# One hybrid mLSTM, convolution and cross-attention layer on one core: the 1152 tokens of a unit in pieces of 256, 512 and 384 columns instead of three times 384

## The chip, the cores and the metric

The kernel runs on 1 core of one Trainium2 chip. The metric is the device time of one execution in microseconds. The profile is of one execution on that core. TensorE's clock has two levels here, 1.2 and 2.4 GHz; the profile gives the granted share (1.00 is 2.4 GHz).

## What is computed

One layer of a streaming encoder, for a prompt of 1024 tokens and 8 sequences of 16 tokens, 1152 tokens of width 1024 in all, in float32. Cut to what matters here:

```python
def layer(x, ...):
    xn = rms_norm(x, g_mix_pre)
    q, k, v, o, ig, fg, glu, xq, gates = jnp.split(xn @ w_in, IN_SPLITS, axis=-1)   # 10248 columns
    y_ml = ...                                        # mLSTM, 4 heads x 256
    y_cv = jax.nn.silu(layer_norm(causal_dwconv(ga * sigmoid(gb), ...)))
    y_xa = mem_attention(xq, mk, mv)                  # into 256 memory tokens
    mixed = (sigmoid(gates[..., 0:D]) * (y_ml @ w_branch[0])
             + sigmoid(gates[..., D:2 * D]) * (y_cv @ w_branch[1])
             + sigmoid(gates[..., 2 * D:]) * (y_xa @ w_branch[2]))
    x = x + rms_norm(mixed @ w_out, g_mix_post)
    fa, fb = jnp.split(rms_norm(x, g_ffn_pre) @ w_ffn_in, 2, axis=-1)               # 2 x 2816 columns
    return x + rms_norm((silu(fa) * fb) @ w_ffn_out, g_ffn_post)
```

## The kernel before

**A unit.** Most products of the layer are done in units: 128 output features for all 1152 tokens. A unit's weights are 8 blocks (`KT`) of 128 by 128, its moving operand the activations `A_hi` and `A_lo`, held as 8 blocks of 128 partitions by 1152 tokens. To keep float32 accuracy, each operand is split into a high and a low part of type fp32r, and three products are summed: high by high, high weights by low activations, low weights by high activations. So a unit is 8 x 3 steps, and since a PSUM bank holds 512 columns, each step is one matmul for each of three pieces of the 1152 tokens: 72 matmuls, every one with its own weight load. `product` (line 256) writes these loops for all but the feed-forward part, where `in_unit` (line 1949) has them.

**Where the units are.** 1 unit for the two mLSTM gates (`pe_proj`, line 745), 80 units of the input projection (`pe_proj`), 3 x 8 units of the branch products (`pe_branch`, line 998), 44 units of the first feed-forward product (`in_unit`). That is 149 units. The feed-forward output (`out_part`, line 1971) and `w_out` (`wo_tile`, line 1923) work on 128 tokens by 512 columns and have another shape. The first phase projects the 256 memory tokens with matmuls of 256 columns, through `product` too (`pe_norm`, line 456).

**PSUM.** `PS` is all 8 banks of 512 columns. Units alternate between banks 0 to 2 and 3 to 5, and each of the three pieces starts at the start of its bank and fills 384 of its 512 columns (`banks`, line 742). The next unit computes while the one before is read out. What reads it takes all three pieces in one instruction, as a pattern of three runs of 384 (`thirds`, line 595): ScalarE's copies and tanhs of the projection (line 677), VectorE's gate products of the branches (lines 1028 and 1040), and in the feed-forward part ScalarE's tanh (line 2043) and VectorE's two products (lines 2162 and 2166).

**Order.** Every engine runs a list written out by hand, and semaphores tie them. `use_unit` (line 265) waits for the low part of the unit's weights (`w_lo_done`, made by POOL at line 253 from ScalarE's high part, line 249) and signals `w_used` with its last matmul. A unit writes its banks once the unit two before it has been read out. Between phases all engines meet (`end_phase`, line 269).

**The first unit of the branches.** The convolution's output goes through a LayerNorm that works on thirds of the tokens, `TC` = 384 columns each (`cut`, line 586). Its low parts are made by three instructions: thirds 0 and 2 by VectorE (`dve_ln`, line 935), third 1 by POOL (`pool_ln`, line 930). `pe_branch` takes the first unit (J = 0) piece by piece, 24 matmuls each: piece 0 waits for third 0, piece 1 for third 1, piece 2 for third 2.

```python
pe.wait_ge((ln_lo, ln_lo_pool, ln_lo)[c], (1, 1, 2)[c])
```

**The first units of the feed-forward part.** `in_unit(0, (0, 1), False)` and `in_unit(1, (0, 1), False)` compute pieces 0 and 1 of two units, and piece 2 follows once the last three tiles of 128 tokens are normalised.

Of the kernel before, what the change touches and what calls it, by code (L numbers as in the profile page):

```python
# [21 lines left out]
ACT = mybir.ActivationFunctionType  # L22
# [3 lines left out]
P = 128  # L26
# [5 lines left out]
NT = NTOK // P  # L32
NPT = SEQ // P
TC = NTOK // 3
H, DH = 4, 256
MEM = 256
CW = 31
# [48 lines left out]
def hybrid_step(nc, a, o):  # L86
    ctx = ExitStack()
    with ctx:
# [503 lines left out]

            return t[j] if isinstance(j, int) else t[bass.ds(j, 1)].rearrange("a p n -> (a p) n")

        def thirds(t):
            return t.rearrange("p (c n) -> p c n", c=3)

        def seg(t, n):

# [68 lines left out]
        def act_proj(act):  # L668
            def lap(i, func, scale, between=()):
                for s in range(RAW):  # L670
                    j = RAW * i + s
                    u = U_PROJ + j
                    split_hi(act, u + SPLIT, U_PROJ // RAW + i + (s + SPLIT) // RAW, (s + SPLIT) % RAW)
                    act.wait_ge(w_used, u + 1)
                    if not isinstance(j, int) or j > 1:
                        act.wait_ge(stage_stored[s % 2], 16 * (2 * i + s // 2))
                    nc.scalar.activation(thirds(stage[:, s % 2]), PS[:, 3 * (s % 2):3 * (s % 2) + 3, 0:TC], func,
                                         scale=scale).then_inc(p_copied, 1)
                    act.wait_ge(p_copied, j + 1)
                    act.dma_start(dtile(proj_d, j), stage[:, s % 2]).then_inc(stage_stored[s % 2], 16)  # L680
                    if s < len(between):
                        between[s](act)
# [51 lines left out]
                    split_lo(pool, U_PROJ + RAW * i + s + SPLIT, (s + SPLIT) % RAW)  # L734

        def a_hi(k, c):
            return A_hi[:, k, TC * c:TC * (c + 1)]

        def a_lo(k, c):
            return A_lo[:, k, TC * c:TC * (c + 1)]  # L740

        def banks(b):
            return [PS[:, 3 * b + c, 0:TC] for c in range(3)]

        def pe_proj(pe):
            pe.wait_ge(wif_lo_done, 1)
# [57 lines left out]
        def dve_proj(dve):  # L804
# [9 lines left out]
            steps.wait()  # L814
            dve.wait_ge(state_m_loaded, 48)
            dve.wait_ge(wif_used, 1)
            steps.mark(nc.vector.tensor_scalar(thirds(g_i[:]), PS[0:H, 3:6, 0:TC], g_bias[0:H, 0:1], None, ALU.add))
            nc.vector.tensor_scalar(thirds(g_f[:]), PS[32:32 + H, 3:6, 0:TC], g_bias[32:32 + H, 0:1], None, ALU.add).then_inc(gate_read, 1)
            dve.wait_ge(gate_read, 1)

            nc.vector.scalar_tensor_tensor(out=g_a[:], in0=g_f[:], scalar=-1.0, in1=g_f[:], op0=ALU.mult, op1=ALU.min).then_inc(g_dve, 1)
# [197 lines left out]
        def dve_branch(dve, n, between=None):  # L1019
            def body(i):  # L1020
                for s in range(RAW):
                    J = KT * n + RAW * i + s
                    lap = 2 * n + i
                    dve.wait_ge(w_used, U_BR + J + 1)
                    dve.wait_ge(gate_loaded[s % 2], 16 * (2 * lap + s // 2 + 1))
                    if not isinstance(J, int) or J > 1:
                        dve.wait_ge(part_stored[s % 2], 16 * (2 * lap + s // 2))
                    nc.vector.scalar_tensor_tensor(out=thirds(part_out[:, s % 2]), in0=thirds(gate_in[:, s % 2]), scalar=1.0,
                                                   in1=PS[:, 3 * (s % 2):3 * (s % 2) + 3, 0:TC], op0=ALU.add,
                                                   op1=ALU.mult).then_inc(part_mul if n else part_done, 1)  # L1030
                    if n:
                        dve.wait_ge(part_mul, J - KT + 1)
                        dve.wait_ge(prev_loaded[s % 2], 16 * (2 * (lap - 2) + s // 2 + 1))
                        nc.vector.tensor_tensor(part_out[:, s % 2], part_out[:, s % 2], prev_in[:, s % 2], ALU.add).then_inc(part_done, 1)

            def merge(k):
                J, b = 2 * KT + k, k % 2
                dve.wait_ge(w_used, U_BR + J + 1)
                dve.wait_ge(gate_loaded[b], 16 * (J // 2 + 1))
                nc.vector.scalar_tensor_tensor(out=thirds(gate2[:, b]), in0=thirds(gate2[:, b]), scalar=1.0,  # L1040
                                               in1=PS[:, 3 * b:3 * b + 3, 0:TC], op0=ALU.add, op1=ALU.mult).then_inc(part_mul, 1)
                dve.wait_ge(part_mul, J - KT + 1)
                dve.wait_ge(prev_loaded[k // 4], 16 * KT)
                nc.vector.tensor_tensor(Y[:, k], Y[:, k], gate2[:, b], ALU.add).then_inc(part_done, 1)
            if n < 2:
                br_laps(dve, n, body)
            else:
                for k in range(KT):
                    if k == KT - 1:
                        between(dve)  # L1050
                    merge(k)
# [870 lines left out]
        def pe_ffn(pe):  # L1922
# [23 lines left out]
                    last = nc.tensor.transpose(PS[:, b + k // 4, P * (k % 4):P * (k % 4 + 1)], Y[:, k, P * t:P * (t + 1)], ident[:])  # L1946
                last.then_inc(n_tx, 1)

            def in_unit(u, thirds_, end):
                pe.wait_ge(w_lo_done, IN_JOB[u] + 1)  # L1950
                pe.wait_ge(n_lo, 3 * thirds_[-1] + 3)
                if u == 0:
                    pe.wait_ge(n_st, NT - 1)
                elif u == 1:
                    pe.wait_ge(n_gn, NT - 1)
                elif u % 2 == 0:
                    pe.wait_ge(f_v, u // 2)
                else:
                    pe.wait_ge(f_g, u // 2)
                    for c in range(1, NC):  # L1960
                        if u == 2 * BASE[c] + 1:
                            pe.wait_ge(y_acc, NT * c - 1)
                for k in range(KT):
                    for n, (w_, m_) in enumerate(((w_hi, A_hi), (w_hi, A_lo), (w_lo, A_hi))):
                        for c in thirds_:
                            last = nc.tensor.matmul(PS[:, 3 * (u % 2) + c, 0:TC], w_[:, u % 2, k], m_[:, k, TC * c:TC * (c + 1)],  # L1966
                                                    start=k == 0 and n == 0, stop=k == KT - 1 and n == 2)
                if end:
                    last.then_inc(w_used, 1)
# [45 lines left out]
        def act_ffn(act):  # L2015
# [23 lines left out]
            def evac(u):  # L2039
                act.wait_ge(w_used, U_F + u + 1)  # L2040
                if u:
                    act.wait_ge(f_lo, u // 2)
                nc.scalar.activation(thirds(vb[:]), PS[:, 0:3, 0:TC], ACT.Tanh, scale=0.5).then_inc(f_th, 1)  # L2043

            def g_hi(m):
                act.wait_ge(f_g, m + 1)
# [83 lines left out]
        def dve_ffn(dve):  # L2130
# [27 lines left out]
            def gate(u):  # L2158
                dve.wait_ge(w_used, U_F + u + 1)
                if u % 2 == 0:  # L2160
                    dve.wait_ge(f_th, u // 2 + 1)
                    nc.vector.scalar_tensor_tensor(out=thirds(vb[:]), in0=thirds(vb[:]), scalar=1.0, in1=PS[:, 0:3, 0:TC], op0=ALU.add,  # L2162
                                                   op1=ALU.mult).then_inc(f_v, 1)
                else:
                    dve.wait_ge(f_v, u // 2 + 1)
                    nc.vector.scalar_tensor_tensor(out=thirds(vb[:]), in0=thirds(vb[:]), scalar=0.5, in1=PS[:, 3:6, 0:TC], op0=ALU.mult,
                                                   op1=ALU.mult).then_inc(f_g, 1)

            def collect(c, t):
# [162 lines left out]
```

## Time and profile before

| | |
|---|---|
| median of 3 runs | 2808.9 us (2807.84 to 2810.91) |
| profiled execution, its own time | 2810.57 us |
| its span | 2808.8 us |
| TensorE matmuls busy | 2686.7 us (96%), 15080 |
| TensorE weight loads busy | 2566.7 us (91%), 15080 |
| VectorE, ScalarE, GpSimd busy | 1087.8, 625.3, 650.2 us |
| mean granted clock | 0.985 |

PE is TensorE's matmuls, PEld its weight loads, which overlap them; DVE is VectorE, ACT ScalarE, POOL GpSimd, SP the engine that issues most transfers. A matmul's row in the profile is longer than the distance to the next one, since matmuls are pipelined: what one costs in a row of many is read from the starts.

### The profile page before, as it was taken

The numbers are of one execution on the slowest core, as the hardware profiler recorded it, in microseconds if no ns is written. First come the engines' busy times: TensorE is split into PE (matmuls) and PEld (weight loads), VectorE is DVE, ScalarE is ACT, GpSimd is POOL, SyncE is SP. The second block draws the span as 40 slices with busy tenths as digits, with TensorE's granted clock in tenths as the row PEclk, the third lists the DMA queues.
The fourth block names the chain that finished last, engine by engine and source line by source line (L and its number), as shares of the span: only waits on it lengthen the run. The fifth ranks groups of instructions, "written<-read, shape, count | busy, mean of one in ns | idle before, by whom it ended". The sixth has DMA issues, their size and how long they took to land.

```text
span 2808.8 us, 37457 instructions
## 1 busy us (share of the span) xinstructions
PE 2686.7 (96%) x15080; PEld 2566.7 (91%) x15080; DVE 1087.8 (39%) x1334; ACT 625.3 (22%) x912; POOL 650.2 (23%) x332
## 2 busy tenths in 40 slices
PE   5899999999999999899998898999999999999998
PEld 5899999999999999898888887988999998989897
DVE  3320199999962222216643342245220211110115
ACT  4331111111113233204521141024211110201021
POOL 5421212222221211221201120140313231404131
PEclk9999999999999999999999999999999999999999
DMA  6422333334252223244565534442202020202013
GB/s 180 144 88 88 106 129 121 110 108 142 91 186 80 96 79 105 98 160 106 135 209 177 175 130 147 163 137 90 75 23 68 29 63 23 68 16 68 13 40 135
DMA packets 286828, 294.96 MB, mean 105 GB/s; under 512 B 11386, under 2 KB 250322, under 8 KB 286704
## 3 DMA queue, kind: packets, MB, share of 16 engines
q1 hardware_dynamic: 271800, 239.91, 27.6%
q10 hardware_dynamic: 14912, 53.48, 4.8%
q8 instruction: 75, 1.23, 0.2%
q14 instruction: 41, 0.34, 0.0%
HBM read 208.27 MB, written 85.55 MB: 105 GB/s over the span
## 4 chain that ended last, share of the span: by engine, by line
PE 49%; issue 39%; POOL 8%; DVE 2%; ACT 1%; DMA 1%; SPq 0%; POOLq 0%; DVEq 0%; ACTq 0%
PE PS L1966 19%; PE PS L261 11%; PE PS L1989 9%; POOL w_lo L253 7%; PE PS L1936 3%; PE PS L1531 1%; PE PS L1550 1%; PE PS L1206 1%; PE PS L1214 1%; PE PS L1172 1%; DVE x_T L536 0%; PE PS L1179 0%; DVE y_T L1369 0%; DMA stage<-in_state_conv 0%; PE PS L1167 0%
## 5 line engine op out<-in xcount | busy, mean ns | idle before, releaser
L261 PE MATMUL PS<-A_hi,w_hi 128*128 128x384 f32 x2496 | 573.4, 336 | 17.3 <-DVE A_lo L935 10.0
L261 PE MATMUL PS<-A_lo,w_hi 128*128 128x384 f32 x2496 | 570.9, 335 | 0.0
L261 PE MATMUL PS<-A_hi,w_lo 128*128 128x384 f32 x2496 | 570.4, 335 | 0.0
L253 POOL TENSOR_TENSOR w_lo<-w_raw,w_hi 128x1024 fp32r<-128x1024 f32 x120 | 306.1, 2554 | 1052.6 <-ACT w_hi L249 1052.6
L261 PEld LDWEIGHTS PS<-A_hi,w_hi 128*128 128x128 f32 x2496 | 446.4, 188 | 20.1 <-issue 17.0
L261 PEld LDWEIGHTS PS<-A_lo,w_hi 128*128 128x128 f32 x2496 | 446.5, 188 | 0.0
L261 PEld LDWEIGHTS PS<-A_hi,w_lo 128*128 128x128 f32 x2496 | 446.2, 188 | 0.0
L890 DVE SCALAR_TENSOR_TENSOR c_out<-ext,taps,c_out 128x1024 f32<-128x1024 f32 x480 | 424.1, 962 | 0.7 <-DVE c_out L890 0.7
L249 ACT CAST w_hi<-w_raw 128x1024 fp32r<-128x1024 f32 x120 | 126.3, 1053 | 1079.2 <-PE PS L261 1071.8
L1966 PE MATMUL PS<-A_hi,w_hi 128*128 128x384 f32 x1056 | 242.5, 334 | 2.8 <-POOL w_lo L1881 2.8
L1966 PE MATMUL PS<-A_lo,w_hi 128*128 128x384 f32 x1056 | 242.3, 334 | 0.0
L1966 PE MATMUL PS<-A_hi,w_lo 128*128 128x384 f32 x1056 | 242.2, 334 | 0.0
L1966 PEld LDWEIGHTS PS<-A_hi,w_hi 128*128 128x128 f32 x1056 | 188.2, 188 | 3.5 <-POOL w_lo L1881 3.1
L1966 PEld LDWEIGHTS PS<-A_lo,w_hi 128*128 128x128 f32 x1056 | 188.4, 188 | 0.0
L1966 PEld LDWEIGHTS PS<-A_hi,w_lo 128*128 128x128 f32 x1056 | 188.4, 188 | 0.0
L1881 POOL TENSOR_TENSOR fo_lo<-w_raw,fo_hi 128x1024 fp32r<-128x1024 f32 x22 | 52.9, 2404 | 412.9 <-ACT fo_hi L1876 412.9
L1881 POOL TENSOR_TENSOR w_lo<-w_raw,w_hi 128x1024 fp32r<-128x1024 f32 x44 | 106.2, 2415 | 151.4 <-ACT w_hi L1876 151.4
L2162 DVE SCALAR_TENSOR_TENSOR vb<-vb,PS 128x1152 f32<-128x1152 f32 x22 | 29.8, 1354 | 272.8 <-ACT vb L2043 272.8
L1989 PE MATMUL PS<-fo_hi,G_hi 128*128 128x512 f32 x396 | 122.7, 391 | 0.0
L1989 PE MATMUL PS<-fo_lo,G_hi 128*128 128x512 f32 x396 | 122.0, 389 | 0.0
L1989 PE MATMUL PS<-fo_hi,G_lo 128*128 128x512 f32 x396 | 122.0, 389 | 0.0
L2173 DVE TENSOR_TENSOR Y_tok<-Y_tok,PS 128x1024 f32<-128x1024 f32 x45 | 54.9, 1221 | 153.6 <-PE PS L1989 153.0
(289 smaller groups left out, 2766.3 us busy)
## 6 DMA issues: line engine op xcount, KB each, us to landing
proj_d<-stage ACTq DMA_DIRECT2D x80, 576.0 KB, 2.7
w_raw<-in_w_in SPq DMA_DIRECT2D x80, 512.0 KB, 4.2
w_raw<-in_w_ffn_in SPq DMA_DIRECT2D x44, 512.0 KB, 3.9
w_raw<-in_w_branch SPq DMA_DIRECT2D x24, 512.0 KB, 4.3
w_raw<-in_w_ffn_out SPq DMA_DIRECT2D x22, 512.0 KB, 3.4
glu<-proj_d SPq DMA_DIRECT2D x16, 576.0 KB, 5.9
gate_in<-proj_d SPq DMA_DIRECT2D x16, 576.0 KB, 6.4
part_d<-part_out SPq DMA_DIRECT2D x16, 576.0 KB, 4.7
```

The source lines that it names most:

```text
L249: nc.scalar.copy(w_hi[:, s % SPLIT, 0:kt], w_raw[:, s, 0:kt]).then_inc(w_hi_done, 1)
L253: nc.gpsimd.tensor_tensor(w_lo[:, s % SPLIT, 0:kt], w_raw[:, s, 0:kt], w_hi[:, s % SPLIT, 0:kt].bitcast(F32), ALU.subtract).then_inc(w_lo_ ...
L261: last = nc.tensor.matmul(out, w[:, k], m(k, c), start=start and k == 0 and n == 0, stop=stop and k == kt - 1 and n == 2)
L890: steps.mark(nc.vector.scalar_tensor_tensor(out=c, in0=src, scalar=tap_scalar(w, k), in1=c, op0=ALU.mult, op1=ALU.add))
L1172: last = nc.tensor.matmul(PS[:, 0, P * h:P * (h + 1)], k_in[:, b, 2 * h + z], q_in[:, b, 2 * h + z], start=z == 0, stop=z == 1)
L1206: last = nc.tensor.matmul(PS[:, 4 + h, 0:E1], q_in[:, b, 2 * h + z], C_T[:, h, z], start=z == 0, stop=z == 1)
L1881: nc.gpsimd.tensor_tensor(l_, job_raw(n), h_.bitcast(F32), ALU.subtract).then_inc(w_lo_done, 1)
L1936: last = nc.tensor.matmul(PS[:, b + z], m_, w_[:, k, 512 * z:512 * (z + 1)], start=k == 0 and n == 0, stop=k == KT - 1 and n == 2)
L1966: last = nc.tensor.matmul(PS[:, 3 * (u % 2) + c, 0:TC], w_[:, u % 2, k], m_[:, k, TC * c:TC * (c + 1)], start=k == 0 and n == 0, stop=k == ...
L1989: last = nc.tensor.matmul(PS[:, b + z], g_[:, k, P * t:P * (t + 1)], w_[:, k, 512 * z:512 * (z + 1)], start=k == 0 and n == 0, stop=k == C ...
L2162: nc.vector.scalar_tensor_tensor(out=thirds(vb[:]), in0=thirds(vb[:]), scalar=1.0, in1=PS[:, 0:3, 0:TC], op0=ALU.add, op1=ALU.mult).then_i ...
L2173: nc.vector.tensor_tensor(Y_tok[:, t], Y_tok[:, t], pair(fo_banks(t)), ALU.add).then_inc(y_acc, 1)
```

## The change

A table `CUTS` gives the borders of the pieces: 0, 256, 768, 1152. The pieces are 256, 512 and 384 tokens wide. In PSUM a unit's 1152 columns lie without a gap: the first piece in the second half of its first bank, the second in the whole second bank, the third in the first 384 columns of the third bank (`wide`). Everything that reads a unit takes one run of 1152 columns. The order of matmuls, their number, their weights and the semaphores stay, but for the numbers in two waits that give the same value. The LayerNorm still works on thirds of 384, and `pe_branch` waits for the same semaphores ahead of its pieces.

```diff
+CUTS = (0, 256, 768, NTOK)
...
-        def thirds(t):
-            return t.rearrange("p (c n) -> p c n", c=3)
+        PS_cols = PS[:].rearrange("p b c -> p (b c)")
+
+        def wide(b):
+
+            return PS_cols[:, 1536 * b + 256:1536 * b + 256 + NTOK]
...
-                    nc.scalar.activation(thirds(stage[:, s % 2]), PS[:, 3 * (s % 2):3 * (s % 2) + 3, 0:TC], func,
+                    nc.scalar.activation(stage[:, s % 2], wide(s % 2), func,
                                          scale=scale).then_inc(p_copied, 1)
...
         def a_hi(k, c):
-            return A_hi[:, k, TC * c:TC * (c + 1)]
+            return A_hi[:, k, CUTS[c]:CUTS[c + 1]]
 
         def a_lo(k, c):
-            return A_lo[:, k, TC * c:TC * (c + 1)]
+            return A_lo[:, k, CUTS[c]:CUTS[c + 1]]
 
         def banks(b):
-            return [PS[:, 3 * b + c, 0:TC] for c in range(3)]
+            return [wide(b)[:, CUTS[c]:CUTS[c + 1]] for c in range(3)]
...
-                    nc.vector.scalar_tensor_tensor(out=thirds(part_out[:, s % 2]), in0=thirds(gate_in[:, s % 2]), scalar=1.0,
-                                                   in1=PS[:, 3 * (s % 2):3 * (s % 2) + 3, 0:TC], op0=ALU.add,
+                    nc.vector.scalar_tensor_tensor(out=part_out[:, s % 2], in0=gate_in[:, s % 2], scalar=1.0,
+                                                   in1=wide(s % 2), op0=ALU.add,
                                                    op1=ALU.mult).then_inc(part_mul if n else part_done, 1)
...
-            def in_unit(u, thirds_, end):
+            def in_unit(u, cuts, end):
                 pe.wait_ge(w_lo_done, IN_JOB[u] + 1)
-                pe.wait_ge(n_lo, 3 * thirds_[-1] + 3)
+                pe.wait_ge(n_lo, CUTS[cuts[-1] + 1] // P)
...
-                        for c in thirds_:
-                            last = nc.tensor.matmul(PS[:, 3 * (u % 2) + c, 0:TC], w_[:, u % 2, k], m_[:, k, TC * c:TC * (c + 1)],
+                        for c in cuts:
+                            last = nc.tensor.matmul(banks(u % 2)[c], w_[:, u % 2, k], m_[:, k, CUTS[c]:CUTS[c + 1]],
                                                     start=k == 0 and n == 0, stop=k == KT - 1 and n == 2)
...
-                nc.scalar.activation(thirds(vb[:]), PS[:, 0:3, 0:TC], ACT.Tanh, scale=0.5).then_inc(f_th, 1)
+                nc.scalar.activation(vb[:], wide(0), ACT.Tanh, scale=0.5).then_inc(f_th, 1)
```

The other readers of a unit (lines 817, 818, 1040, 2162 and 2166) are rewritten in the same way.

## Rows read from the trace of the kernel before

**Rows 1.** The page: busy time of the engines, and the granted clock in 40 slices

```profile
PE 2686.7 (96%) x15080; PEld 2566.7 (91%) x15080; DVE 1087.8 (39%) x1334; ACT 625.3 (22%) x912; POOL 650.2 (23%) x332
...
PEclk9999999999999999999999999999999999999999
```

**Rows 2.** Groups of instructions, shapes apart: name, count | busy us, mean ns | idle before

```profile
L261 PE MATMUL PS<-A_hi,w_hi 128*128 128x384 f32 x2496 | 573.4, 336 | 17.3 <-DVE A_lo L935 10.0 <-POOL A_lo L1690 4.3 <-POOL A_lo L1353 1.8
...
L1966 PE MATMUL PS<-A_hi,w_hi 128*128 128x384 f32 x1056 | 242.5, 334 | 2.8 <-POOL w_lo L1881 2.8
```

**Rows 3.** Timeline of TensorE's matmuls in the projection: start us, length us

```profile
599.79 0.68 PE L261 MATMUL PS<-A_hi,w_hi 128*128 128x384 f32 x3
...
605.51 0.68 PE L261 MATMUL PS<-A_hi,w_lo 128*128 128x384 f32 x3
```

**Rows 4.** The same timeline in the feed-forward output

```profile
2339.73 0.62 PE L1989 MATMUL PS<-fo_lo,G_hi 128*128 128x512 f32 x2
...
2343.36 0.62 PE L1989 MATMUL PS<-fo_hi,G_hi 128*128 128x512 f32 x2
```

**Rows 5.** The same timeline in the memory projection, clock at 2.4 GHz

```profile
94.03 0.28 PE L261 MATMUL PS<-mem_lo,w_hi 128*128 128x256 f32 x1
...
95.21 0.28 PE L261 MATMUL PS<-mem_hi,w_lo 128*128 128x256 f32 x1
...
95.78 0.29 PE L261 MATMUL PS<-mem_hi,w_lo 128*128 128x256 f32 x1
...
96.73 0.28 PE L261 MATMUL PS<-mem_lo,w_hi 128*128 128x256 f32 x1
96.86 0.28 PE L261 MATMUL PS<-mem_hi,w_lo 128*128 128x256 f32 x1
96.97 0.28 PE L261 MATMUL PS<-mem_hi,w_hi 128*128 128x256 f32 x1
97.09 0.28 PE L261 MATMUL PS<-mem_lo,w_hi 128*128 128x256 f32 x1
```

**Rows 6.** The same timeline where the clock is at 1.2 GHz

```profile
74.83 0.41 PE L261 MATMUL PS<-mem_hi,w_hi 128*128 128x256 f32 x1
...
76.53 0.41 PE L261 MATMUL PS<-mem_hi,w_lo 128*128 128x256 f32 x1
```

**Rows 7.** Weight loads of the projection, as a group

```profile
L261 PEld LDWEIGHTS PS<-A_lo,w_hi 128*128 128x128 f32 x2496 | 446.5, 188 | 0.0
```

**Rows 8.** Groups of ScalarE and VectorE that read a unit, and like ones

```profile
L677 ACT ACTIVATE stage<-PS 128x1152 f32<-128x1152 f32 x80 | 90.1, 1126 | 0.0
...
L2049 ACT CAST G_hi<-vb 128x1152 fp32r<-128x1152 f32 x22 | 25.6, 1162 | 17.6 <-DVE vb L2166 17.6
...
L1028 DVE SCALAR_TENSOR_TENSOR part_out<-gate_in,PS 128x1152 f32<-128x1152 f32 x16 | 21.7, 1355 | 154.1 <-PE PS L261 154.1
...
L2147 DVE SCALAR_TENSOR_TENSOR Y<-PS,r_y,post 128x1024 f32<-128x1024 f32 x9 | 11.5, 1276 | 0.7 <-POOL r_y L2092 0.7
```

**Rows 9.** Who waited for whom: us in total, times, longest

```profile
ACT w_hi L249 <- PE PS L261: 1071.8, 105, 29.5
```

**Rows 10.** Timeline of the first branch unit, TensorE

```profile
1149.70 0.66 PE L261 MATMUL PS<-A_hi,w_hi 128*128 128x384 f32 x1 [9.98 <-DVE A_lo L935]
1150.15 0.52 PE L261 MATMUL PS<-A_lo,w_hi 128*128 128x384 f32 x1
...
1154.95 0.52 PE L261 MATMUL PS<-A_lo,w_hi 128*128 128x384 f32 x1
...
1156.44 0.33 PE L261 MATMUL PS<-A_hi,w_lo 128*128 128x384 f32 x1
1156.62 0.33 PE L261 MATMUL PS<-A_hi,w_hi 128*128 128x384 f32 x1
```

**Rows 11.** Timelines of POOL and VectorE beside it

```profile
1148.86 7.40 POOL L930 TENSOR_TENSOR A_lo<-cT,A_hi 128x3072 fp32r<-128x3072 f32 x1 [5.59 <-ACT A_hi L926]
```

```profile
1151.47 8.00 DVE L935 TENSOR_TENSOR A_lo<-cT,A_hi 128x3072 fp32r<-128x3072 f32 x1 [1.87 <-ACT A_hi L926]
1165.14 1.35 DVE L1028 SCALAR_TENSOR_TENSOR part_out<-gate_in,PS 128x1152 f32<-128x1152 f32 x1 [5.66 <-PE PS L261]
```

More of the change, by code:

```diff
@@ L816, in dve_proj @@
             dve.wait_ge(wif_used, 1)
-            steps.mark(nc.vector.tensor_scalar(thirds(g_i[:]), PS[0:H, 3:6, 0:TC], g_bias[0:H, 0:1], None, ALU.add))
-            nc.vector.tensor_scalar(thirds(g_f[:]), PS[32:32 + H, 3:6, 0:TC], g_bias[32:32 + H, 0:1], None, ALU.add).then_inc(gate_read, 1)
+            steps.mark(nc.vector.tensor_scalar(g_i[:], wide(1)[0:H], g_bias[0:H, 0:1], None, ALU.add))
+            nc.vector.tensor_scalar(g_f[:], wide(1)[32:32 + H], g_bias[32:32 + H, 0:1], None, ALU.add).then_inc(gate_read, 1)
             dve.wait_ge(gate_read, 1)
@@ L1039, in merge @@
                 dve.wait_ge(gate_loaded[b], 16 * (J // 2 + 1))
-                nc.vector.scalar_tensor_tensor(out=thirds(gate2[:, b]), in0=thirds(gate2[:, b]), scalar=1.0,
-                                               in1=PS[:, 3 * b:3 * b + 3, 0:TC], op0=ALU.add, op1=ALU.mult).then_inc(part_mul, 1)
+                nc.vector.scalar_tensor_tensor(out=gate2[:, b], in0=gate2[:, b], scalar=1.0,
+                                               in1=wide(b), op0=ALU.add, op1=ALU.mult).then_inc(part_mul, 1)
                 dve.wait_ge(part_mul, J - KT + 1)
@@ L2161, in gate @@
                     dve.wait_ge(f_th, u // 2 + 1)
-                    nc.vector.scalar_tensor_tensor(out=thirds(vb[:]), in0=thirds(vb[:]), scalar=1.0, in1=PS[:, 0:3, 0:TC], op0=ALU.add,
+                    nc.vector.scalar_tensor_tensor(out=vb[:], in0=vb[:], scalar=1.0, in1=wide(0), op0=ALU.add,
                                                    op1=ALU.mult).then_inc(f_v, 1)
@@ L2165, in gate @@
                     dve.wait_ge(f_v, u // 2 + 1)
-                    nc.vector.scalar_tensor_tensor(out=thirds(vb[:]), in0=thirds(vb[:]), scalar=0.5, in1=PS[:, 3:6, 0:TC], op0=ALU.mult,
+                    nc.vector.scalar_tensor_tensor(out=vb[:], in0=vb[:], scalar=0.5, in1=wide(1), op0=ALU.mult,
                                                    op1=ALU.mult).then_inc(f_g, 1)
```

## The prediction

> **What bounds the kernel now.** I read the busy times first: TensorE's matmuls fill 96% of the span, no other engine has over 39%, and the granted clock stands at 2.4 GHz in nearly all slices [rows 1]. Then the groups: the matmuls of 384 columns, 2496 + 1056 of each of the three forms, are most of it, and almost nothing idles before them [rows 2]. Then the waits, for the direction of the dependence: ScalarE waits for TensorE 1071.8 us, 105 times, to split the next weights [rows 9]. So the readers and splitters are hidden, and the kernel's time is the number of matmuls times the distance between their starts. That distance decides this change, and I read it from the timeline.
>
> **The matmuls.** In the projection 33 matmuls of 384 columns start in 605.51 - 599.79 = 5.72 us, 173.3 ns each [rows 3]. In the feed-forward output 16 matmuls of 512 columns start in 3.63 us, 226.9 ns each [rows 4]. Between the two lie 53.6 ns for 128 columns, which is 0.42 ns a column, the array's own pace at 2.4 GHz; 384 columns alone would be 160 ns, so each matmul pays about 13 ns beside its columns. If a matmul of 256 pays the same, it takes 173.3 - 53.6 = 119.7 ns. The change leaves the number of matmuls and of columns as they are, so a constant addition cancels: 119.7 + 226.9 + 173.3 = 519.9 ns for three pieces, against 3 x 173.3 = 519.9 ns now.
>
> There is one direct row for 256 columns. In the memory projection, with the same weight loads and the same fp32r type, the starts are 1.18 us / 10 = 118 ns and 1.31 us / 11 = 119.1 ns apart [rows 5]. So the 256 piece may be 0.6 to 1.7 ns cheaper than the straight line says. There are 2496 + 1056 triples by the groups, and 24 in the gate unit, which stands under other names: 3576. I take 119 ns, the longer stretch, 0.7 ns under the line: 3576 x 0.7 = **-2.5 us**. The bounds are 118 ns (-6.1 us) and 119.7 ns (0). This is the whole change for the steady stretches, and it is delicate: each ns on a triple is 3.6 us, or 0.13% of the time.
>
> At 1.2 GHz there is no addition to distribute: 256 columns take 1.70 us / 8 = 212.5 ns [rows 6] and 384 columns 4.80 us / 15 = 320 ns [rows 10], both columns over clock. Nothing changes there.
>
> **The first branch unit.** It is the one place where the pieces differ in what they wait for. Now piece 0 starts at 1149.70 after a hole, its 24 matmuls run mostly at 1.2 GHz, the last starts at 1156.44, and piece 1 follows at 1156.62 without a wait [rows 10], since POOL's low part for it was done at 1148.86 + 7.40 = 1156.26 [rows 11]. With 256 columns piece 0 takes 24 x 0.2125 = 5.1 us and 0.1 for the slow first start: it ends at 1154.9. Piece 1, now 512 columns, needs thirds 0 and 1 and so still waits for POOL until 1156.3. Then 24 x 0.2269 + 24 x 0.1733 = 9.6 us, and VectorE's third 2 (done 1151.47 + 8.00 = 1159.47) is early for piece 2. The end is 1165.9 in place of 1156.62 + 48 x 0.1733 = 1164.9: **+1.0 us**. Upper bound: the pause of 1.4 us keeps the clock at 1.2 GHz through piece 1, which then costs 24 x (427 - 227) ns = 4.8 us more (427 being 512 columns at the 0.83 ns a column of rows 6 and 10). I keep +1.0, because the clock in rows 10 rose after 5.6 us of work, and piece 0 is about as long; the lower bound is 0.
>
> The first two feed-forward units wait for the same six token tiles ahead of pieces 0 and 1 (256 + 512 = 2 x 384) and for nine ahead of piece 2: nothing.
>
> **The readers.** ScalarE's read of a unit takes 1126 ns as three runs of 384; a plain run of 1152, from SBUF, takes 1162 ns. VectorE's product takes 1355 ns for 1152 in three runs and 1276 for 1024 columns out of two whole banks [rows 8], 0.62 ns for each column more; a run is not visibly dearer for being broken in three. So I expect within 50 ns of the present lengths. They are hidden behind the 12.5 us (72 x 173.3 ns) of the next unit. Where the cover is gone, at the end of the projection and of each branch, four reads lie on the path: 4 x 0.05 = 0.2 us either way at most, taken as 0. Were a read twice as long, it would still end 10 us ahead of need. The banks used are the same six, so no matmul gets a new wait.
>
> **Sum.** -2.5 + 1.0 = -1.5 us, against the profiled execution's 2810.6 us: 2809.1 us. That execution was 1.7 us above the median; against the median it is 2807.4 us, which I forecast.
>
> **Rivals.**
>
> 1. *The short matmul is cheaper still in the mixture (faster).* For: the starts of the 256 matmuls are uneven (the last four of rows 5 lie 0.13, 0.11 and 0.12 us apart), so what makes up the 13 ns is not simply a constant; it vanishes at 1.2 GHz. If in a triple the 256 piece pays nearer to 10 ns, the triple loses 3 ns: -10.7 + 1.0 = -9.7 us, 2799 us. From -1.9 ns a triple on the change counts as faster. Against: the 384 and 512 rows pay the same addition to a fraction of a ns, and they are two of the three pieces.
>
> 2. *The weight load behind the short matmul shows (slower).* Every matmul has its own load of 128 by 128, whose row is 188 ns long [rows 7] and which must be under way during the matmul before. Behind 384 columns it has 173 ns, behind the 256 piece only 119. In the mixture the matmul that follows it is the longest, and if its weights come late by a few ns, each triple pays. It decides from +1.3 ns a triple. For: the unevenness of the 256 starts looks like a load and a stream of nearly equal length that miss each other. Against: in rows 5 every matmul has only 118 to 119 ns for its load and keeps that pace, so a load in steady flow fits. Price: the row's 188 ns cannot all be exposed, as rows 5 exclude it; the single starts there swing by a few ns about their mean, and if 3 ns of that become a loss, +10.7 + 1.0 = +11.7 us, 2821 us.
> The Trainium skill ("TensorE: Matmul & The Clock Gate", LDWEIGHTS) gives a load as columns over 1.2 GHz, which is an estimate of 107 ns for 128 columns, exactly the stream time of 256 columns at 2.4 GHz. By that rule the load behind a 256 piece has no slack beyond the matmul's own addition, but it fits in 119 ns, so the sum would stay as it is; the 188 ns of the trace's row are longer than the rule's figure, and no row shows a load by itself.
>
> 3. *The change doesn't touch the time at all.* The pieces are renamed and the additions cancel exactly: +1.0 us or less for the branch unit, 2809 to 2810 us. It lies within the forecast.
>
> **How the numbers follow.** A measurement of this kernel can tell about 0.2% (5.6 us) from no change. The forecast, with rival 3 inside it: 0.50, its own range 2802 to 2811 us. Rival 1: 0.27. Rival 2: 0.23. The range for 8 in 10 reaches into both: low 2798 (rival 1 at -3.3 ns a triple), high 2821 (rival 2 at its price). Chances: faster 0.27, same 0.50, slower 0.23.
>
> **What would show it.** In the changed profile: the starts of a triple 119, 227 and 173 ns apart, and a unit of 12.46 to 12.48 us. The forecast is wrong if the start after the 256 piece comes later than 121 ns (rival 2) or before 117 ns (rival 1), or if the 384 or 512 piece has another distance than in rows 3 and 4. In the first branch unit, a wait of about 1.4 us for POOL between pieces 0 and 1. The readers at 1.08 to 1.18 us on ScalarE and 1.3 to 1.4 us on VectorE. And TensorE must show no wait for a reader.

## The result, and the profile after

The changed kernel takes 2844.8 us (median of 4 runs, 2842.46 to 2849.85) against 2808.4 us before, a ratio of 1.013 with a 95% interval of 1.0113 to 1.0148. The forecast was 2807.4 us, no change, with a range of 2798 to 2821 us; the measured time is 24 us above the top of the range. The profiled execution has a span of 2843.4 us (2808.8 before).

The page of the changed kernel, busy time of the engines, and the granted clock (its first slice is an 8, where it was a 9):

```profile
PE 2718.9 (96%) x15080; PEld 2433.6 (86%) x15080; DVE 1083.8 (38%) x1334; ACT 624.3 (22%) x912; POOL 649.1 (23%) x332
...
PEclk8999999999999999999999999999999999999999
```

The share and the number of matmuls are as before [rows 1]; nothing new stands in between. The weight loads' share is 86% where it was 91%, but it is 86% too in a later run of the same sizes that loses nothing, so it doesn't tell where the time went. The groups of instructions, shapes apart, show one new wait, the one for POOL that the forecast named (1.5 us ahead of the 512 piece); those ahead of the 256 piece stood ahead of the first piece before [rows 2]:

```profile
L262 PE MATMUL PS<-A_hi,w_hi 128*128 128x512 f32 x832 | 329.4, 396 | 1.5 <-POOL A_lo L934 1.5
...
L262 PE MATMUL PS<-A_hi,w_hi 128*128 128x256 f32 x832 | 239.1, 287 | 17.6 <-DVE A_lo L939 10.0 <-POOL A_lo L1694 4.3 <-POOL A_lo L1357 2.2
...
L681 ACT ACTIVATE stage<-PS 128x1152 f32<-128x1152 f32 x80 | 90.1, 1126 | 0.0
```

ScalarE's read of a unit is 1126 ns in one run as in three [rows 8].

Where the time went is seen in the timeline of the projection. Each row is one step, three matmuls, of the changed kernel (start, length):

```profile
610.16 0.69 PE L262 MATMUL PS<-A_hi,w_hi 128*128 128x256 f32 x3
610.69 0.70 PE L262 MATMUL PS<-A_lo,w_hi 128*128 128x256 f32 x3
611.23 0.68 PE L262 MATMUL PS<-A_hi,w_lo 128*128 128x256 f32 x3
611.75 0.51 PE L262 MATMUL PS<-A_hi,w_hi 128*128 128x256 f32 x2
```

The steps start 0.53, 0.54 and 0.52 us apart, where the kernel before has 0.52 each time [rows 3]. By the single starts of the trace, the piece of 256 takes 117, 127 or 118 ns, that of 512 takes 231, 239 or 232, that of 384 178, 174 or 171, over and over, and three steps together 1587 ns where 3 x 520 = 1560 were. Over 480 steps the means are 120.8, 233.9 and 174.2 ns. The chain of waits gives it for eight units (576 matmuls of the feed-forward part; start, length). Before, then after:

```profile
2214.80 99.86 PE PS L1966 x576
```

```profile
2242.91 101.54 PE PS L1970 x576
```

So a unit is (101.54 - 99.86) / 8 = 0.21 us longer, and by the starts 12.693 against 12.480 us, in every phase. Of the 149 units, 142 run through like this at 2.4 GHz: 142 x 0.213 = **30.2 us** of the 34.6 by which the spans differ. The other seven are the gate unit, the first unit of each branch and the first three of the feed-forward part.

The first branch unit, TensorE, at the border of pieces 0 and 1, and POOL beside it:

```profile
1165.91 0.55 PE L262 MATMUL PS<-A_hi,w_hi 128*128 128x256 f32 x1 [9.98 <-DVE A_lo L939]
...
1172.52 0.50 PE L262 MATMUL PS<-A_hi,w_hi 128*128 128x512 f32 x1 [1.51 <-POOL A_lo L934]
1172.86 0.39 PE L262 MATMUL PS<-A_lo,w_hi 128*128 128x512 f32 x1
```

```profile
1165.07 7.40 POOL L934 TENSOR_TENSOR A_lo<-cT,A_hi 128x3072 fp32r<-128x3072 f32 x1 [5.58 <-ACT A_hi L930]
```

```profile
1182.45 1.35 DVE L1032 SCALAR_TENSOR_TENSOR part_out<-gate_in,PS 128x1152 f32<-128x1152 f32 x1 [6.76 <-PE PS L262]
```

From its first start to its reader it takes 1182.45 - 1165.91 = 16.5 us; it took 1165.14 - 1149.70 = 15.4 [rows 10, 11]. That is the forecast's +1.0 us, with the wait for POOL that it named (1.4 us there, 1.5 here). Most of the rest lies where the clock was at 1.2 GHz for another stretch than before: the mean granted clock is 0.983 against 0.985. In the third feed-forward unit, after the same wait of 2.78 us, the kernel before ran its second step at the 2.4 GHz pace and the changed one at the 1.2 GHz pace (0.96 us a step). Before, then after:

```profile
2003.17 0.81 PE L1966 MATMUL PS<-A_hi,w_hi 128*128 128x384 f32 x3 [2.78 <-POOL w_lo L1881]
2003.81 0.69 PE L1966 MATMUL PS<-A_lo,w_hi 128*128 128x384 f32 x3
2004.34 0.68 PE L1966 MATMUL PS<-A_hi,w_lo 128*128 128x384 f32 x3
```

```profile
2027.73 1.33 PE L1970 MATMUL PS<-A_hi,w_hi 128*128 128x256 f32 x3 [2.78 <-POOL w_lo L1885]
2028.86 1.16 PE L1970 MATMUL PS<-A_lo,w_hi 128*128 128x256 f32 x3
2029.82 1.04 PE L1970 MATMUL PS<-A_hi,w_lo 128*128 128x256 f32 x3
```

By the starts this unit is 1.4 us longer, the first unit of the second branch 1.7 and that of the third 0.4, and the gate unit is 1.0 us shorter. With the 1.1 us of the first branch unit and the 30.2 us that makes 33.8 of the 34.6 us.

And the same first branch unit holds a hint: there the pieces run apart, 24 of one size in a row, and the 512 pieces start 227 ns apart and the 384 pieces 173, as in rows 3 and 4 (the 256 pieces ran at 1.2 GHz, nearly all). The places in PSUM are those of the change, yet nothing is lost. So the loss looks to be in the mixture.

### The profile page after: what moved, and what is told of

Same layout as the page of the kernel before. It is cut to its first block, busy times and chain, and to the rows that moved or that the text cites. A ratio compares the mean times of both kernels' runs of the same rounds, so it can differ in the third digit from the quotient of the medians.

```text
span 2843.4 us, 37457 instructions
## 1 busy us (share of the span) xinstructions
PE 2718.9 (96%) x15080; PEld 2433.6 (86%) x15080; DVE 1083.8 (38%) x1334; ACT 624.3 (22%) x912; POOL 649.1 (23%) x332
## 4 chain that ended last, share of the span: by engine, by line
PE 49%; issue 39%; POOL 8%; DVE 2%; ACT 1%; DMA 1%; SPq 0%; POOLq 0%; DVEq 0%; ACTq 0%
PE PS L1970 20%; PE PS L262 11%; PE PS L1993 9%; POOL w_lo L254 7%; PE PS L1940 3%; PE PS L1535 1%; PE PS L1554 1%; PE PS L1210 1%; PE PS L1218 1%; PE PS L1176 1%; DVE x_T L537 0%; PE PS L1183 0%; DMA wif<-in_w_in 0%; DVE y_T L1373 0%; PE PS L1171 0%
## 5 line engine op out<-in xcount | busy, mean ns | idle before, releaser
L262 PE MATMUL PS<-A_hi,w_hi 128*128 128x256 f32 (+2 forms) x2496 | 581.5, 340 | 19.1 <-DVE A_lo L939 10.0
L262 PE MATMUL PS<-A_lo,w_hi 128*128 128x256 f32 (+2 forms) x2496 | 582.4, 341 | 0.0
L262 PE MATMUL PS<-A_hi,w_lo 128*128 128x256 f32 (+2 forms) x2496 | 578.0, 339 | 0.0
L262 PEld LDWEIGHTS PS<-A_hi,w_hi 128*128 128x128 f32 x2496 | 403.1, 189 | 59.6 <-issue 17.2
L262 PEld LDWEIGHTS PS<-A_lo,w_hi 128*128 128x128 f32 x2496 | 406.6, 189 | 37.5
L262 PEld LDWEIGHTS PS<-A_hi,w_lo 128*128 128x128 f32 x2496 | 404.2, 189 | 39.3
L1970 PE MATMUL PS<-A_lo,w_hi 128*128 128x256 f32 (+2 forms) x1056 | 249.8, 342 | 0.0
L1970 PE MATMUL PS<-A_hi,w_hi 128*128 128x256 f32 (+2 forms) x1056 | 245.0, 338 | 2.8 <-POOL w_lo L1885 2.8
L1970 PE MATMUL PS<-A_hi,w_lo 128*128 128x256 f32 (+2 forms) x1056 | 244.0, 337 | 0.0
L1970 PEld LDWEIGHTS PS<-A_lo,w_hi 128*128 128x128 f32 x1056 | 174.4, 188 | 15.0
L1970 PEld LDWEIGHTS PS<-A_hi,w_lo 128*128 128x128 f32 x1056 | 171.1, 188 | 17.6
L1970 PEld LDWEIGHTS PS<-A_hi,w_hi 128*128 128x128 f32 x1056 | 169.4, 188 | 19.1 <-POOL w_lo L1885 3.1
L2166 DVE SCALAR_TENSOR_TENSOR vb<-vb,PS 128x1152 f32<-128x1152 f32 x22 | 29.8, 1354 | 278.7 <-ACT vb L2047 278.7
L2170 DVE SCALAR_TENSOR_TENSOR vb<-vb,PS 128x1152 f32<-128x1152 f32 x22 | 29.8, 1355 | 220.6 <-PE PS L1970 220.6
```

Of the source, the lines that this page charges most:

```text
L262: last = nc.tensor.matmul(out, w[:, k], m(k, c), start=start and k == 0 and n == 0, stop=stop and k == kt - 1 and n == 2)
L1970: last = nc.tensor.matmul(banks(u % 2)[c], w_[:, u % 2, k], m_[:, k, CUTS[c]:CUTS[c + 1]], start=k == 0 and n == 0, stop=k == KT - 1 and n ...
L2166: nc.vector.scalar_tensor_tensor(out=vb[:], in0=vb[:], scalar=1.0, in1=wide(0), op0=ALU.add, op1=ALU.mult).then_inc(f_v, 1)
L2170: nc.vector.scalar_tensor_tensor(out=vb[:], in0=vb[:], scalar=0.5, in1=wide(1), op0=ALU.mult, op1=ALU.mult).then_inc(f_g, 1)
```

## The experiments

Three theories to begin with. **A**: it is the alternation of unequal sizes that costs. **B**: the 256 piece doesn't cover the weight load behind it (rival 2). **C**: writing from the middle of a PSUM bank costs.

**Pieces one after the other.** In the changed kernel the loop over pieces goes outside:

```diff
-            for k in range(kt):
-                for n, (w, m) in enumerate(((wh, mh), (wh, ml), (wl, mh))):
-                    for c, out in enumerate(outs):
+            for c, out in enumerate(outs):
+                for k in range(kt):
+                    for n, (w, m) in enumerate(((wh, mh), (wh, ml), (wl, mh))):
```

(and the same in `in_unit`)

> The changed kernel with its loops turned: for each unit first all 24 matmuls of the 256 piece, then the 24 of the 512 piece, then the 24 of the 384 piece. Same sizes, same places in PSUM, same weights, same number of matmuls and loads; only the neighbours differ. A (the alternation of sizes costs): starts 118 to 119, 227 and 173 ns apart, a unit of about 12.46 us, a total of 2804 to 2809 us, the loss gone. B (the 256 piece doesn't cover the load behind it): each 256 matmul still has a load in its 119 ns; loss of the same size, 2840 to 2845 us, unless a load can be late only behind a piece that follows a longer one. C (writing the second half of a bank is slow): loss stays on the 256 piece, 2840 us or more.

Measured: 2818.1 us, ratio to before 1.0026 (1.0016 to 1.0036). The chain of waits has for eight feed-forward units:

```profile
2218.71 100.16 PE PS L1970 x576
```

100.16 - 99.86 = 0.30 us for eight units, by the starts 12.520 us each, 0.04 over the kernel before. So 0.173 of the 0.213 us a unit are gone with the mixture, some 25 of the 30 us, although each 256 piece still has only 120 ns for a load: B in its plain form and C fall, as far as this kernel goes. What is left stands at the changes of size: the first six or so matmuls after each are uneven (170, 175, 178, 185, 176, 181 ns for 384) before they settle at 173 or 174. The time is 9 us above A's range: 0.04 us in 149 units are 6 of them, and the kernel before took 2811.1 us beside this run, 2.7 above its median at the start.

**Equal pieces at column 128 of each bank.**

```diff
-            return [PS[:, 3 * b + c, 0:TC] for c in range(3)]
+            return [PS[:, 3 * b + c, 128:512] for c in range(3)]
```

(and in all readers and in `in_unit`)

> The kernel before with its three equal pieces of 384 put in the last 384 columns of their banks, so that every matmul and every reader starts at column 128 of a bank. A and B: no change, a unit of 12.48 us, 2808 us. C (a start in the middle of a bank costs): each matmul pays 3 ns or more, a unit of 12.7 us, 2840 us or more.

Measured: 2812.5 us in one run, the kernel before 2811.1 beside it; a unit 12.480 us. A start at column 128 costs nothing. C is out.

**320, 512, 320.** The waits for the LayerNorm's thirds and the token tiles are fitted to the pieces:

```diff
-CUTS = (0, 256, 768, NTOK)
+CUTS = (0, 320, 832, NTOK)
...
-            return PS_cols[:, 1536 * b + 256:1536 * b + 256 + NTOK]
+            return PS_cols[:, 1536 * b + 192:1536 * b + 192 + NTOK]
...
-                            pe.wait_ge((ln_lo, ln_lo_pool, ln_lo)[c], (1, 1, 2)[c])
+                            for third in range(-(-CUTS[c + 1] // TC)):
+                                pe.wait_ge((ln_lo, ln_lo_pool, ln_lo)[third], (1, 1, 2)[third])
```

> The changed kernel with the pieces 320, 512 and 320 (borders 0, 320, 832, 1152; unit starts at column 192 of its first bank). The shortest piece streams 133 ns, longer than the 118 ns in which a chain of 256 pieces takes its loads. A: the alternation costs all the same, a unit of 12.6 to 12.8 us, 2830 to 2850 us. B: the load is covered, a unit of 12.48 us, 2808 us (perhaps 1 or 2 us more for the first branch unit, whose second piece now waits for the last third). C: loss as in the change, since its first piece starts in the middle of a bank.

Measured: 2841.8 us, a unit of 12.640 us:

```profile
2241.29 101.11 PE PS L1971 x576
```

No piece is under 320 columns, and the loss is 0.16 us a unit. B would have it gone. A holds. The units make 149 x 0.16 = 23.8 of the 30.7 us over the kernel before; 3.8 more are a second wait for VectorE in the first branch unit (13.8 against 10.0 us in all), since piece 1 now reaches into the last third. The rest is not traced.

**384, 512, 256.** The same edit with borders 384 and 896 and the unit at column 128.

> The changed kernel with its pieces in another order and place: 384, 512, 256 (borders 0, 384, 896, 1152; the 256 piece now starts at the start of the third bank, the 384 piece at column 128 of the first). A and B: about the loss of the change, a unit of 12.6 to 12.8 us, 2835 to 2850 us; A leaves open where it shows, by B the interval behind the 256 piece (now that of 384) is the late one. C (a 256 piece in the second half of a bank): the loss is gone, 2808 us.

Measured: 2815.3 us in one run, the kernel before 2811.1; the second wait for VectorE (13.5 against 10.0 us) is 3.5 of the difference. A unit of 12.480 us:

```profile
2219.59 99.86 PE PS L1971 x576
```

The same three sizes, mixed, and no loss in a unit. Neither A nor B expected that; C did, but C had fallen. So either the order of the sizes decides (theory **O**), or where each piece lies (**P**). The next two runs cross them. In `product` and `in_unit` the steps issue their pieces in the other order:

```diff
-                    for c, out in enumerate(outs):
-                        last = nc.tensor.matmul(out, w[:, k], m(k, c), start=start and k == 0 and n == 0,
+                    for c in ((2, 1, 0) if len(outs) == 3 else range(len(outs))):
+                        last = nc.tensor.matmul(outs[c], w[:, k], m(k, c), start=start and k == 0 and n == 0,
```

> The changed kernel, pieces and places as in the change (256 in the second half of its bank, 512, 384), but each step issues them in the order 384, 512, 256. O (the cyclic order of the sizes decides: 256 to 512 to 384 loses, 384 to 512 to 256 does not): a unit of 12.48 us, 2809 to 2815 us. P (the place in PSUM or in the activations decides): a unit of 12.69 us as in the change, 2840 to 2845 us.

> The pieces and places of the 384, 512, 256 run, issued in the order 256, 512, 384. O: the loss comes back, a unit of 12.69 us, about 2843 us. P: none, a unit of 12.48 us, 2815 us.

Measured: the change with its order turned 2811.7 us, ratio to before 1.0006 (0.9996 to 1.0015), a unit of 12.480 us. The other layout turned to 256, 512, 384: 2852.1 us in one run, a unit of 12.693 us, the change's own number (its total is 7 us above the change's; its second wait for VectorE explains only a part of that). The chain of waits of the changed kernel with its order turned:

```profile
2216.06 99.86 PE PS L1970 x576
```

O is shown. Issued as 256, 512, 384 the unit loses 0.213 us in either layout, issued as 384, 512, 256 it loses nothing in either, with the same matmuls, loads, places and readers. It is a cheap repair of the change, one line in each of the two loops, and it ends level with the kernel before, not ahead. The two sums were not made of fixed terms either: 384, 512, 256 adds up to 520 ns as 174, 229 and 116 in one layout and as 168, 236 and 116 in the other, by the starts.

**Blocks of one mixture.** To see the rule behind it, blocks of 24 extra steps were put behind the gate unit of the kernel before, where the other engines and the transfers leave TensorE alone (from 180 us to the end of the blocks no other engine is busy, and the DMA share is 0.00). Their results are not used. The loop of the second and third of these runs:

```diff
             product(banks(1), wif_hi, wif_lo, a_hi, a_lo, KT).then_inc(wif_used, 1)
+            pe.wait_ge(w_lo_done, U_PROJ + 1)
+            for pieces, M in MEASURED:
+                for k in range(KT):
+                    for n, (w, m) in enumerate(((w_hi, A_hi), (w_hi, A_lo), (w_lo, A_hi))):
+                        for c, (size, at_, src) in enumerate(pieces):
+                            nc.tensor.matmul(PS[0:M, c, at_:at_ + size], w[:, 0, k, 0:M], m[:, k, src:src + size],
+                                             start=k == 0 and n == 0, stop=k == KT - 1 and n == 2)
```

The first such run took the gate unit's weights (`wif_hi`, `wif_lo`):

> The kernel before with sixteen blocks of 72 extra matmuls right behind the gate unit, when no other engine and no transfer is busy; their results are not used. Each block is one sequence of sizes, 24 steps of three, all outputs at the start of a bank unless said: 384 x 3; 256, 512, 384; the same with the change's place in PSUM; 384, 512, 256; both mixed orders with all pieces read from token 0; 256, 512, 384 and 384, 512, 256 and 384 x 3 with weights of 64 columns; 352, 416, 384; 512, 512, 128; 448, 512, 192; 320, 512, 320; 256 x 3; and 256, 512, 384 and 384 x 3 in plain fp32. O: 12.69 us for every 256, 512, 384 block with 128 weight columns, 12.48 for 384, 512, 256, whatever the places. P: the block with the change's place in PSUM, or those with the pieces' own places in the activations, differ from their like. L (the length of the weight load matters): with 64 weight columns the mixed block comes down to the equal one. If any inequality costs, 352, 416, 384 costs too; if only a short piece costs, it doesn't. [...] The whole program is about 16 x 12 to 25 us longer: 3020 to 3080 us.

Measured (ns a step, mean of the second half of a block, from the single starts): 384 x 3 524; 256-512-384 533, and 533 again with the change's place in PSUM and 533 with all pieces read from token 0; 384-512-256 520 and 520; with 64 weight columns 522, 525 and 523 for the two orders and the equal pieces; 320-512-320 523; 352-416-384 527; 448-512-192 544; 512-512-128 576; 256 x 3 353.6, which is 117.9 ns each; plain fp32 1935 for the mixed block and 1935 for the equal one. So O again, and nothing from the places. With the load half as long the mixed blocks lie within 2 ns of the equal one, and with a stream 3.7 times as long (1935 against 520) there is no difference. But the equal block ran at 524 here and a row of 256 at 117.9 each, where the kernel before has 520 and the straight line 120. The block of 256, its first row and the first of the next block:

```profile
296.31 0.52 PE L775 MATMUL PS<-A_hi,wif_hi 128*128 128x256 f32 x3
...
304.80 1.02 PE L775 MATMUL PS<-A_hi,wif_hi 128*128 128x256 f32 x3
```

The gate unit itself, ahead of the blocks, shows more. It has equal pieces, and its matmuls, weights and places are the same in the kernel before, in this run and in the next. Six steps of it at 2.4 GHz take 3.18, 3.14 and 3.12 us, 530, 523 and 520 ns a step. The three traces in this order:

```profile
124.70 0.69 PE L261 MATMUL PS<-A_hi,wif_hi 128*128 128x384 f32 x3
...
127.88 0.34 PE L261 MATMUL PS<-A_hi,wif_hi 128*128 128x384 f32 x1
```

```profile
124.29 0.69 PE L281 MATMUL PS<-A_hi,wif_hi 128*128 128x384 f32 x3
...
127.43 0.69 PE L281 MATMUL PS<-A_hi,wif_hi 128*128 128x384 f32 x3
```

```profile
124.49 0.68 PE L286 MATMUL PS<-A_lo,wif_hi 128*128 128x384 f32 x3
...
127.61 0.68 PE L286 MATMUL PS<-A_lo,wif_hi 128*128 128x384 f32 x3
```

So with these weights one and the same row of equals settles at more than one distance, up to 10 ns a step apart; what chooses is not shown. With the projection's weights every steady unit of equal pieces has 520. The next runs use those.

> The kernel before with extra blocks of 24 steps behind the gate unit, now with the projection's own weights (first unit) and all outputs at the start of a bank; results not used. One size repeated: 128, 192, 256, 384, 512; three sizes in turn: 256-512-384, 384-512-256, 512-512-128, 448-512-192, 192-512-448, 320-512-320, 352-416-384, 384-416-352, 256-512-256, 256-256-384; two in turn: 256-512, 256-384, 384-512; and with shorter loads: 256-512-384 with 64 and with 96 weight columns, 384 x 3 with 64. Theory now, E: a load of 128 columns takes L of about 107 to 120 ns and can't start before the matmul ahead of its own has; a piece that streams less than L exposes the rest. E says: 128 repeated runs at L, about 107 to 120 ns a matmul, not at 67; 192 repeated the same, 107 to 120, not at 93; 256 and longer pay only 13 ns; the triples with 128 and 192 lose 50 and 25 ns in either order; 64 or 96 weight columns take the loss of 256-512-384 away. Order (O) says beside it: 256-512-384 at 529 to 533 ns a triple and 384-512-256 at 520, and tells by the pairs whether what counts is the matmul ahead of the 256 or the one behind it: if 256-512 loses and 256-384 doesn't, it is the longer one behind. If instead every mixture of unequal sizes loses (rival M), 352-416-384, 384-512 and 256-384 all lose 3 ns or more a matmul.

> Blocks as in the run before, now for the length of the load. 384-512 in turn with 128, 96, 64 and 32 weight columns; 256-512-384 with 112, 64 and 32; 384-416-352 and 352-416-384 with 64; 448-512-192 and 512-512-128 with 64; 128 repeated with 96 and 64, 192 repeated with 64, 224 repeated with 128; all pieces read from token 8 on for 384 x 3, 256-512-384 and 384-512-256; 384-480-288 and 288-480-384 with 128. E (two effects of the weight load: its floor of 112 ns, and a loss in mixtures that it makes while it runs beside the stream): both shrink with its columns. 384-512 loses 13 ns with 128 columns, about 0 to 7 with 96, under 3 with 64 and 32; the mixtures with 64 columns all lie within 3 ns of columns plus 13 ns a matmul; 448-512-192 and 512-512-128 with 64 columns lose under 5 ns, where they lost 24 and 57; 128 repeated runs at about 84 ns with 96 columns and at 67 or a little less with 64; 224 repeated with 128 columns at 112 ns. A (the alternation of stream lengths alone, loads apart): 384-512 keeps its 13 ns with 32 columns too. If where the activations start matters, token 8 changes the three blocks against 520, 529 and 520.

Measured, over the second half of a block or its repeating pattern. "Straight" is columns / 2.4 GHz plus 13.3 ns for each matmul, the line through rows 3 and 4:

```
sizes in turn         weight columns   ns a step   straight   over
384 384 384                128           520.0       520.0      0.0
512 512 512                128           680.0       680.0      0.0
256 256 256                128           360.0       360.0      0.0
224 224 224                128           335.0       320.0     15.0
192 192 192                128           335.0       280.0     55.0
128 128 128                128           335.0       200.0    135.0
256 512                    128           346.7       346.7      0.0
256 384                    128           293.3       293.3      0.0
256 512 256                128           466.7       466.7      0.0
256 256 384                128           410.0       413.3     -3.3
384 512                    128           413.3       400.0     13.3
384 512 256                128           520.0       520.0      0.0
256 512 384                128           528.9       520.0      8.9
320 512 320                128           526.7       520.0      6.7
352 416 384                128           526.7       520.0      6.7
384 416 352                128           533.3       520.0     13.3
288 480 384                128           523.3       520.0      3.3
384 480 288                128           523.3       520.0      3.3
192 512 448                128           543.3       520.0     23.3
448 512 192                128           544.4       520.0     24.4
512 512 128                128           576.9       520.0     56.9
256 512 384             112/96/64/32     526.7 523.3 518.3 520.0    6.7 3.3 -1.7 0.0
384 512                  96/64/32        403.3 403.3 406.7          3.3 3.3 6.7
384 416 352                 64           520.0       520.0      0.0
352 416 384                 64           520.0       520.0      0.0
448 512 192                 64           516.7       520.0     -3.3
512 512 128                 64           516.7       520.0     -3.3
128 128 128               96/64          255.0 180.0 200.0     55.0 -20.0
192 192 192                 64           265.8       280.0    -14.2
```

With all three pieces read from token 8 on, where the table's triples read each from its own place (0, 384, 768 for the equal ones): 384 x 3 530.0, 256-512-384 523.3, 384-512-256 523.3. Two kinds of blocks were in both runs and agree within 1 ns: 384-512 with 128 weight columns (413) and 256-512-384 with 64 (518 and 519).

The blocks with 128 weight columns of one short size, in the timeline of the first of these runs (each row is the first of a block; the next row's start ends it):

```profile
292.20 0.44 PE L778 MATMUL PS<-A_hi,w_hi 128*128 128x128 f32 x3
...
300.19 0.53 PE L778 MATMUL PS<-A_hi,w_hi 128*128 128x192 f32 x3
...
308.26 0.54 PE L778 MATMUL PS<-A_hi,w_hi 128*128 128x256 f32 x3
...
316.92 0.86 PE L778 MATMUL PS<-A_hi,w_hi 128*128 128x512 f32 x3
```

72 matmuls of 128 columns take 7.99 us and 72 of 192 columns 8.07 us, 111 and 112 ns each whatever they stream; those of 256 take 120 ns. That is a floor, and it goes with the weight columns: in the second run

```profile
256.40 0.34 PE L777 MATMUL PS<-A_hi,w_hi 128*64 128x128 f32 x3
...
260.72 0.43 PE L777 MATMUL PS<-A_hi,w_hi 128*64 128x192 f32 x3
...
267.10 0.39 PE L777 MATMUL PS<-A_hi,w_hi 128*96 128x128 f32 x3
...
273.20 0.74 PE L777 MATMUL PS<-A_hi,w_hi 128*128 128x384 f32 x3
```

128 columns with 96 weight columns take 6.10 / 72 = 85 ns, with 64 they take 4.32 / 72 = 60 ns. With 64 weight columns no floor shows: 192 columns take 6.38 / 72 = 89 ns there, 29 more than 128 do. The floor is the load: 112 ns for 128 weight columns. The Trainium skill ("TensorE: Matmul & The Clock Gate", LDWEIGHTS) gives a load as columns over 1.2 GHz, which makes an estimate of 107 and 80 ns for 128 and 96; the trace agrees within 5 ns.

And two blocks that bear on rival 2, 384-512 in turn and, with short loads, 256-512-384:

```profile
282.29 0.57 PE L778 MATMUL PS<-A_hi,w_hi 128*128 128x384 f32 x2
...
292.20 0.44 PE L778 MATMUL PS<-A_hi,w_hi 128*128 128x128 f32 x3
...
333.26 0.69 PE L778 MATMUL PS<-A_hi,w_hi 128*64 128x256 f32 x3
...
345.70 0.68 PE L778 MATMUL PS<-A_hi,w_hi 128*64 128x384 f32 x3
```

9.91 us / 24 = 413 ns a pair, 13 over the straight line, with no piece short of the load; and 12.44 us / 24 = 518 ns a step for the change's own mixture once its loads have 64 columns.

What follows:

- *Two different losses.* Under about 256 columns a piece no longer covers the load behind it, and the step pays the rest, in any order: about 24 ns with a piece of 192, which was run in two orders, and 57 with one of 128 (the load's 112 less 80 and 53 ns of stream are 32 and 59). With 64 weight columns both are gone, as E said.
- *The change's loss is the other one.* It appears without a short piece (384-512: 13.3; 384-416-352: 13.3), is absent with one (256-512 and 256-384: 0), and depends on the order. It is there in the blocks, where no transfer and no reader runs, so they are not its cause. In the change's mixture it shrinks as the load does, 8.9, 6.7, 3.3, -1.7 ns with 128, 112, 96 and 64 weight columns, which points to the load having a part in it. E's "under 3 ns" for all short loads fell: the pair 384-512 keeps 3.3 ns with 64 and 6.7 with 32. Single blocks that differ by a few ns prove little, since a row of equals was seen 10 ns a step apart with nothing changed; the order's 8.9 ns stand on some 140 units of each kernel.
- *It is a settled pattern, and there can be several.* Most mixtures fall into a pattern that repeats exactly after one to three steps. That is what a load and a stream would look like that disturb one another by their relative position; what they share is not shown by any run here. Read from token 8 the equal pieces ran at 530 and the change's mixture at 523, against 520 and 529; but the gate unit's equal pieces ran at 530 from token 0 as well, so that the place of the operands did it is not shown.

**512, 512, 128 in the whole kernel**, with the edit of 320, 512, 320 and the unit at column 0 of its first bank:

> The whole kernel with the pieces 512, 512 and 128 (unit starts at the start of its first bank). E, from the block's 576.9 ns a triple: a unit of 24 x 0.5769 = 13.85 us in place of 12.48, 149 units: +204 us, 3010 to 3020 us. If the blocks don't carry over to the kernel with its transfers and readers, another value; if only the place of the 256 piece had mattered, 2810 us.

Measured: 3029.6 us, a unit of 12.48 + 1.38 = 13.86 us: the block's number carries over. The total is 10 us above the top of the forecast; 6.8 of them are in the waits of TensorE, since piece 0 of the first branch unit now needs POOL's third as well:

```profile
PE PS L262 <- POOL A_lo L934: 16.8, 1, 16.8
```

against 10.0 us for VectorE's third before [rows 10].

## Why the prediction was wrong

- *What bounds the kernel*: right. TensorE without a gap, time = number of matmuls times the distance of their starts. The readers and the waits did nothing, as said.
- *"A constant addition cancels: 119.7 + 226.9 + 173.3 = 519.9 ns"*: this is the step that failed. Each of the three distances was right for a row of equals with the projection's weights: the blocks give 120.0, 226.7 and 173.3 to a tenth. But the addition of 13.3 ns is not a property of a size that can be summed over a mixture. In the order 256, 512, 384 it comes to 528.9 ns a step, and 7.2 of the 8.9 ns too many stand at the 512 piece (233.9 in place of 226.7), the sign that the prediction had named for being wrong. The term "3576 x 0.7 = -2.5 us" measured some +30 us.
- *"I take 119 ns"*: there is no one value for a row of 256. With the projection's weights it settles at 120.0, the straight line's value, with the gate unit's it holds 117.9 through a block of 72. So the uneven 118 to 119 ns of rows 5 may have been a settled row too. A choice of 0.7 ns between them was below what such rows can carry.
- *The first branch unit*: right in mechanism and size, +1.1 us with a 1.5 us wait.
- *The readers*: right, 1126 ns and 1355 ns unchanged.
- *Rival 2* had the direction and a total of 2821 us, too small by 24. Its mechanism, the load exposed behind the 256 piece, shows only below 256 columns; at 256 the load of 112 ns fits into 120, as rows 5 said. The loss is of another kind: it comes and goes with the order of the same pieces.
- *Rival 1* has little for it: with loads of 128 columns, the block 256-256-384 ran 3.3 ns a step under the line, and 256 x 3 with the gate unit's weights 6.4 under; the change's mixture ran over it.
- The range was too narrow for what I knew: the bounds came from rows of equals, and no row of the profile had sizes in turn. With each ns a step worth 3.6 us, an unmeasured mixture deserved more than 3 ns.

## What to carry to other kernels

A distance between matmuls that was read from a row of equal ones holds for rows of equal ones. If a change makes a dense fp32r stream alternate between sizes, measure the exact cycle, in its order, before counting columns; and if it loses, try the other cyclic order first, since here it gave back the whole 1.3%. Keep each piece above the load (112 ns for 128 weight columns here, 256 columns and more), and prefer equal pieces when nothing else speaks against them. Read a row's distance in the phase that you mean to change: equal pieces of 384 ran at 520 ns a step in all units with the projection's weights, and at 520 to 530 in the gate unit.

## What the runs showed of the hardware that was not expected

- The cyclic order of three sizes is worth 0.213 us in 12.48 us: 256-512-384 steps at 528.9 ns, 384-512-256 at 520.0, with everything else the same. With the gate unit's weights it is 533 against 520.
- Matmuls of one size settle at columns / 2.4 GHz + 13.3 ns (120.0, 173.3, 226.7 ns) in fp32r with a load of 128 columns each from the projection's weights, and need some six matmuls after a change of size to do so. The Trainium skill ("TensorE: Matmul & The Clock Gate", Back-to-back issue gap) has 2.5 ns in place of 13.3, for the gap of a single matmul at this clock; the trace differs, and the measurement decides for these fp32r streams.
- The same row of equal matmuls can settle at more than one distance: the gate unit's 384 pieces ran at 530, 523 and 520 ns a step in three kernels that are the same up to there, a row of 256 at 117.9 ns with its weights and at 120.0 with the projection's.
- A load of 128 weight columns sets a floor of 112 ns a matmul, one of 96 a floor of 85 ns.
